# A head's four attention products as split fp32r products among the gate projection's matmuls

## What is computed

```
h = rms_norm(x, attn_norm_g);  proj = h @ w_in      # q,k,v of both kinds, index parts, g_sb, g_ds
# stick-breaking heads
z = q_sb k_sb^T * scale;  mask = key < query
a = where(mask, exp(log_sigmoid(z) + suffix_sum(where(mask, log_sigmoid(-z), 0))), 0)
o_sb = a v_sb
# indexed sparse heads: 64 selected keys of each query
p = softmax(where(selected and causal, qd kd^T * scale, -inf));  o_ds = p v_ds
merged = sigmoid(g_sb) * (o_sb @ w_branch[:1024]) + sigmoid(g_ds) * (o_ds @ w_branch[1024:])
x = x + merged @ w_out;  x = x + MLP(rms_norm(x, ffn_norm_g))
```

## Time and profile before

| | us |
|---|---|
| median of 3 runs | 1435.22 (1435.05 to 1436.7) |
| profiled execution | 1435.36 |
| its span, first to last instruction | 1433.5 |
| PE busy | 1428.1 (100%) |
| DVE busy | 1140.3 (80%) |
| ACT busy | 841.6 (59%) |
| POOL busy | 447.8 (31%) |
| the gates stage: head 0's first chunk begins | at 329.9 |

### The profile page before, as it was taken

One profiled execution on the slowest core, in us unless ns is written; L12 is line 12 of the kernel. 1 busy time (PEld: TensorE's weight loads), 2 busy tenths in 40 slices (PEclk: granted clock), 3 DMA queues, 4 the chain that ended last, 5 costly groups with the idle time before them and its releaser, 6 DMA issues.

```text
span 1433.5 us, 23730 instructions
## 1 busy us (share of the span) xinstructions
PE 1428.1 (100%) x7626; PEld 1223.7 (85%) x7626; DVE 1140.3 (80%) x1533; ACT 841.6 (59%) x1181; POOL 447.8 (31%) x493
## 2 busy tenths in 40 slices
PE   9999999999999999999999999999999999999999
PEld 7888888888888888888888888888888888888887
DVE  6778998886656566899967778777778778999998
ACT  7545667666767666666664455455554545465553
POOL 2310000333132213650025455655556555200000
PEclk9999999999999999999999999999999999999999
DMA  8665665665555555567666666666666665576664
GB/s 255 191 196 173 210 194 183 197 176 176 161 162 158 168 171 178 188 222 233 191 178 182 186 199 182 186 191 190 191 191 180 185 195 189 192 230 206 202 209 147
DMA packets 121064, 272.26 MB, mean 190 GB/s; under 512 B 10688, under 2 KB 10976, under 8 KB 121008
## 3 DMA queue, kind: packets, MB, share of 16 engines
q1 hardware_dynamic: 119936, 268.99, 60.7%
q0 software_dynamic: 896, 2.42, 0.6%
q10 hardware_dynamic: 176, 0.14, 0.0%
HBM read 269.42 MB, written 2.10 MB: 189 GB/s over the span
## 4 chain that ended last, share of the span: by engine, by line
PE 98%; DVE 1%; DMA 0%; issue 0%; ACT 0%; SPq 0%; DVEq 0%; ACTq 0%
PE bank L2086 97%; DVE lo L1215 0%; DMA raw<-in_w_in 0%; PE bank L2140 0%; PE bank L2359 0%; PE bank L2400 0%; DVE y L1758 0%; PE bank L2223 0%; DVE msum L1234 0%; ACT hi L720 0%; SPq L550 0%; DVE msum L1243 0%; DVE msum L1240 0%; DVE lo L1098 0%; ACT hi L637 0%
## 5 line engine op out<-in xcount | busy, mean ns | idle before, releaser
L1098 DVE TENSOR_TENSOR lo<-raw,hi 128x1024 fp32r<-128x1024 f32 (+1 forms) x342 | 444.3, 1304 | 167.1 <-ACT hi L637 166.5
L637 ACT ACTIVATE hi<-raw 128x1024 fp32r<-128x1024 f32 (+1 forms) x342 | 359.2, 1053 | 272.0 <-PE bank L2086 263.8
L2086 PE MATMUL bank<-h2T,hi 128*128 128x512 f32 x1408 | 483.3, 394 | 0.0
L2086 PE MATMUL bank<-h2T,lo 128*128 128x256 f32 x1408 | 376.8, 278 | 0.0
L2086 PEld LDWEIGHTS bank<-h2T,hi 128*128 128x128 f32 x1408 | 257.9, 188 | 53.5
L2086 PE MATMUL bank<-hT,hi 128*128 128x512 f32 (+1 forms) x784 | 272.8, 394 | 0.1
L2086 PEld LDWEIGHTS bank<-h2T,lo 128*128 128x128 f32 x1408 | 264.5, 188 | 7.8
L2086 PE MATMUL bank<-hT,lo 128*128 128x256 f32 (+1 forms) x784 | 212.6, 281 | 0.0
L2050 POOL TENSOR_TENSOR u<-u,rms_row 128x256 f32<-128x256 f32 x88 | 120.8, 1373 | 184.8 <-DVE u L1610 165.8
L2086 PE MATMUL bank<-hi,ffT 128*128 128x512 f32 x576 | 177.3, 389 | 0.0
L2086 PEld LDWEIGHTS bank<-hT,hi 128*128 128x128 f32 (+1 forms) x784 | 143.9, 187 | 29.7 <-DVE lo L1098 0.3
(11 more groups left out here) (298 smaller groups left out, 2023.8 us busy)
## 6 DMA issues: line engine op xcount, KB each, us to landing
raw<-in_w_up SPq DMA_DIRECT2D x176, 512.0 KB, 3.9
raw<-in_w_in SPq DMA_DIRECT2D x160, 512.0 KB, 3.7
raw<-in_w_down SPq DMA_DIRECT2D x88, 512.0 KB, 4.5
raw<-in_w_branch SPq DMA_DIRECT2D x32, 512.0 KB, 3.6
raw<-in_w_out SPq DMA_DIRECT2D x24, 512.0 KB, 5.0
raw4h<-in_w_in SPq DMA_DIRECT2D x8, 512.0 KB, 3.6
raw5h<-in_w_in SPq DMA_DIRECT2D x8, 512.0 KB, 4.0
y<-in_x SPq DMA_DIRECT2D x4, 512.0 KB, 6.5
```

What stands on the lines that cost most here:

```text
L637: act.activation(hi[s][:, 0:width], raw[s][:, 0:width], ACT.Copy)\
L1098: dve.tensor_tensor(lo[s][:, 0:width], raw[s][:, 0:width], hi[s][:, 0:width].bitcast(f32), ALU.subtract)\
L2086: return pe.matmul(o, l, r, start=start, stop=stop, skip_group_check=True)
```

## The change

The four products with fp32 operands become products of fp32r halves, three matmuls in place of each. For this DVE makes the halves: `qk_split(h)` of q and k of both kinds (one copy and one subtraction over 4 x 256 elements; for head 0 ahead of the loop, for head h + 1 in iteration j = 4 of head h), `v_split` (2 x 256 elements, j = 0), `stick_split` (384, ahead of the `lo` of j = 5), `probT_lo` (384, out of PSUM, ahead of the `lo` of j = 6; ACT's `probT` becomes the hi half). POOL no longer copies v, stages into one tile `qk_raw`, and `stage_ds` moves ahead of the mask of `stick`. On PE the blocks behind chunk 0 and chunk 7 go; `cols_chunk` calls `between(k)`, k = 0 to 7, in the middle and at the end of each column tile. In chunk 0 k = 0 to 5 are the scores and logits, in chunk 7 k = 0 to 2 are the first and 5 to 7 the second product with v; each part is one 256-wide and one 128-wide fp32r matmul. The parts at k = 0 wait for the halves. Left out of the diff: semaphore names, and the new `between` parameter in the head of `cols_chunk`.

```diff
@@ -241,15 +241,15 @@
         sin_i = at("sin_i", [TH, 2 * IHALF], A0 + 3968)
         bias = at("bias", [KEYS], A0 + 4096)
         scores = at("scores", [KEYS], A0 + 5632)
-        probT = at("probT", [KEYS], A0 + 5632)
+        probT = at("probT", [KEYS], A0 + 5632, f32r)
 
         W0 = A0 + 7 * KB
         part = [at(f"part{i}", [S], W0 + i * KB) for i in range(4)]
-        sb_q = at("sb_q", [S], W0 + 4 * KB)
-        sb_k = at("sb_k", [S], W0 + 5 * KB)
-        ds_qk = at("ds_qk", [2 * S], W0 + 6 * KB)
-        sb_v = at("sb_v", [TH, HD], W0 + 8 * KB)
-        ds_v = at("ds_v", [TH, HD], W0 + 9 * KB)
+        qk_raw = at("qk_raw", [4, S], W0 + 4 * KB)
+        qk_hi = at("qk_hi", [4, S], 44 * KB, f32r)
+        qk_lo = at("qk_lo", [4, S], 48 * KB, f32r)
+        v_hi = at("v_hi", [2, TH, HD], W0 + 8 * KB, f32r)
+        v_lo = at("v_lo", [2, TH, HD], 52 * KB, f32r)
         partb = [at(f"partb{i}", [S], W0 + (4 + i) * KB) for i in range(4)]
         rms_row = at("rms_row", [S], A0 + 17 * KB)
         one = at("one", [P], A0 + 18 * KB)
...
@@ -317,6 +317,9 @@
         stick = at("stick", [KEYS], 64 * KB + 3072)
         logit = at("logit", [KEYS], 64 * KB + 4608)
         prob = at("prob", [KEYS], 64 * KB + 6144)
+        stick_lo = at("stick_lo", [KEYS], 64 * KB, f32r)
+        stick_hi = at("stick_hi", [KEYS], 64 * KB + 1536, f32r)
+        probT_lo = at("probT_lo", [KEYS], 64 * KB + 6144, f32r)
 
         sig = [[at(f"sig{b}{i}", [S], (32 + 4 * b + i) * KB) for i in range(4)] for b in range(2)]
         br = [[at(f"br{b}{i}", [S], (40 + 4 * b + i) * KB) for i in range(4)] for b in range(2)]
...
@@ -1468,9 +1477,44 @@
             dve.tensor_scalar(bias[:, :], scores[:, :], (NONCAUSAL + TAKEN) / 2, MASKED,
                               ALU.is_gt, ALU.mult).then_inc(bias_raw, 1)
 
-            def gates_body(h):
+            def qk_split(h):
+
+                dve.wait_ge(staged_qk, 3 * h + 3)
+                dve.tensor_copy(qk_hi[:, :, :], qk_raw[:, :, :]).then_inc(qk_hi_done, 1)
+                dve.wait_ge(qk_hi_done, h + 1)
+                dve.tensor_tensor(qk_lo[:, :, :], qk_raw[:, :, :], qk_hi[:, :, :].bitcast(f32),
+                                  ALU.subtract).then_inc(qk_lo_done, 1)
+
+            def v_split(h):
+
+                both = tok[:, 0:4:3, :, ds(HD * h, HD)]
+                dve.tensor_copy(v_hi[:, :, :, :], both).then_inc(v_hi_done, 1)
+                dve.wait_ge(v_hi_done, h + 1)
+                dve.tensor_tensor(v_lo[:, :, :, :], both, v_hi[:, :, :, :].bitcast(f32),
+                                  ALU.subtract).then_inc(v_lo_done, 1)
+
+            def stick_split(h):
+
+                dve.wait_ge(stick_done, h + 1)
+                dve.tensor_copy(stick_hi[:, :], stick[:, :]).then_inc(stick_hi_done, 1)
+                dve.wait_ge(stick_hi_done, h + 1)
+                dve.tensor_tensor(stick_lo[:, :], stick[:, :], stick_hi[:, :].bitcast(f32),
+                                  ALU.subtract).then_inc(stick_lo_done, 1)
+
+            def gates_body(h, more):
                 for j in range(CPG):
+                    if j == 5:
+                        stick_split(h)
+                    if j == 6:
+                        dve.wait_ge(probT_done, h + 1)
+                        dve.tensor_tensor(probT_lo[:, :], B[3][:, 0:KEYS],
+                                          probT[:, :].bitcast(f32), ALU.subtract)\
+                            .then_inc(probT_lo_done, 1)
                     split(C_GATES + AHEAD + j, h, CPG // SLOTS)
+                    if j == 0:
+                        v_split(h)
+                    if j == 4 and more:
+                        qk_split(h + 1)
                     if j == 1:
 
                         dve.wait_ge(logit_full, h + 1)
@@ -1505,8 +1549,10 @@
                                       oT[:, ds(at_head, 1), 0:S].bitcast(f32), ALU.subtract)\
                         .then_inc(done, 1)
 
-            with dve.Fori(0, NH) as h:
-                gates_body(h)
+            qk_split(0)
+            with dve.Fori(0, NH - 1) as h:
+                gates_body(h, True)
+            gates_body(NH - 1, False)
 
             def merged_lo(n, ct):
...
@@ -1949,15 +1995,15 @@
 
             def stage_sb(h):
 
-                pool.tensor_tensor(sb_k[:, :].unsqueeze(1), qkT[:, ds(h, 1), S:2 * S],
+                pool.tensor_tensor(qk_raw[:, 1:2, :], qkT[:, ds(h, 1), S:2 * S],
                                    sb_scale[:, :].unsqueeze(1).to_broadcast([P, 1, S]),
                                    ALU.mult).then_inc(staged_qk, 1)
-                pool.tensor_copy(sb_q[:, :].unsqueeze(1), qkT[:, ds(h, 1), 0:S])\
+                pool.tensor_copy(qk_raw[:, 0:1, :], qkT[:, ds(h, 1), 0:S])\
                     .then_inc(staged_qk, 1)
 
             def stage_ds(h):
-                pool.tensor_copy(ds_qk[:, :].unsqueeze(1), qkT[:, ds(NH + h, 1), :])\
-                    .then_inc(staged_qk, 1)
+                pool.tensor_copy(qk_raw[:, 2:4, :].rearrange("p (n a) s -> p n (a s)", n=1),
+                                 qkT[:, ds(NH + h, 1), :]).then_inc(staged_qk, 1)
 
             with pool.Fori(0, 3) as i:
                 gains_body(i)
@@ -1974,10 +2020,6 @@
                                channel_multiplier=1).then_inc(bias_done, 1)
 
             def head_body(h, more):
-
-                pool.wait_ge(ds_full, 1 + h)
-                pool.tensor_copy(sb_v[:, :, :], tok[:, 0, :, ds(HD * h, HD)]).then_inc(staged_v, 1)
-                pool.tensor_copy(ds_v[:, :, :], tok[:, 3, :, ds(HD * h, HD)]).then_inc(staged_v, 1)
 
                 wait_alone(pool, stay_raw, h + 1)
                 pool.affine_select(out=diagonal(stay), in_=diagonal(stay), compare_op=ALU.is_gt,
@@ -1991,12 +2033,11 @@
 
                     pool.wait_ge(logit_full, h + 1)
                     stage_sb(h + 1)
+                    stage_ds(h + 1)
                 wait_alone(pool, stick_raw, h + 1)
                 pool.affine_select(out=diagonal(stick), in_=diagonal(stick), compare_op=ALU.is_gt,
                                    fill=0.0, base=0, pattern=[[0, 2], [1, P]],
                                    channel_multiplier=-1).then_inc(stick_done, 1)
-                if more:
-                    stage_ds(h + 1)
 
             pool.wait_ge(col_scaled, 4)
...
@@ -2126,9 +2167,14 @@
                                last and j == CK - 1)
                         if first and j == 0:
                             mm(bank[ct][:, 0:S], wl[:, j, cs], src[:, kt, 0:S], False, False)
+                        if between is not None and j == 0:
+                            between(2 * ct)
                     if last and ct < 3:
                         i.then_inc(full, 1)
-                i.then_inc(w_used, 1)
+                    if ct == 3:
+                        i.then_inc(w_used, 1)
+                    if between is not None:
+                        between(2 * ct + 1)
 
             def transposes(k, kts, src, bank=B):
 
@@ -2365,25 +2411,64 @@
             with pe.Fori(1, 4) as i:
                 heads_body(i)
 
+            def split_product(out_, left, right, part, first):
+
+                (l_hi, l_lo), (r_hi, r_lo) = left, right
+                return mm(out_, l_lo if part == 1 else l_hi, r_lo if part == 2 else r_hi,
+                          first and part == 0, part == 2)
+
+            def qk(n, cols):
+                return qk_hi[:, n, cols], qk_lo[:, n, cols]
+
+            def scores_part(h, k):
+
+                old, new, every = slice(0, P), slice(P, S), slice(0, S)
+                if k == 0:
+                    pe.wait_ge(qk_lo_done, h + 1)
+                    pe.wait_ge(qkT_done, 8)
+                if k < 3:
+                    split_product(B[0][:, 0:S], qk(1, old), qk(0, every), k, True)
+                    i = split_product(B[0][:, S:KEYS], qk(1, new), qk(0, new), k, False)
+                    if k == 2:
+                        i.then_inc(z_full, 1)
+                elif k < 6:
+                    split_product(B[1][:, 0:P], qk(2, old), qk(3, old), k - 3, True)
+                    i = split_product(B[1][:, P:KEYS], qk(2, new), qk(3, every), k - 3, False)
+                    if k == 5:
+                        i.then_inc(logit_full, 1)
+
+            def values_part(h, k):
+
+                def product(bank, n, w_hi, w_lo, part):
+                    v = [(v_hi[:, n, t, :], v_lo[:, n, t, :]) for t in range(TH)]
+                    split_product(bank[:, 0:S], v[0], (w_hi[:, 0:S], w_lo[:, 0:S]), part, True)
+                    return split_product(bank[:, P:S], v[1],
+                                         (w_hi[:, S:KEYS], w_lo[:, S:KEYS]), part, False)
+
+                if k == 0:
+                    pe.wait_ge(v_lo_done, h + 1)
+                    pe.wait_ge(stick_lo_done, h + 1)
+                    pe.wait_ge(sb_done, 1 + h)
+                if k < 3:
+                    i = product(B[2], 0, stick_hi, stick_lo, k)
```

(45 more changed lines are left out.)

## The result

The changed kernel takes 1449.0 us (median of 5 runs, 1448.59 to 1450.18) against 1435.22 (5 runs too): ratio 1.0095, 95% interval 1.0084 to 1.0107. That is slower, inside the range and on the forecast's side, 3.5 us above the forecast. The profiled execution is 1448.59, its span 1446.9: +13.4 us on the span of before.

The account below looks back on a forecast made before the run. PE was taken to bound the kernel, by what it issues plus what it waits. Start wait 3.4, products 0.6 and head waits 6.4 gave +10.4 on 1435.36, forecast as 1445.5 us, range 1438.5 to 1449.5.

Parts of the forecast that it names:

- The start wait: Gates stage start: PE's first part waits once for DVE's split of q and k, 3.4 us (3.9 with slow copy).
- The wait in each head: Before each head's transposes: PE waits for POOL's scaling of `prob`, 0.8 us a head, 6.4 in all.
- the step: In each head: PE gives chunk 0 back 1.35 us later, while the transposes' own turn moves by only 0.04.
- Rival B: In the heads POOL gets in before DVE's `lo`, so transposes are just in time; 1439.3 us, chance 0.22.
- The price of the products: On PE, twelve parts of 0.225 us replace fp32 blocks of 2.63: +0.07 a head, +0.6 us in all.
- the upper bound of +0.19: Parts' price on PE if a narrow product costs 0.12 us: +0.19 a head, +1.5 us in all.
- Rival C: On PE weight loads hide, a narrow product costs 0.06; 1434.5 us (chance 0.05), or 1440.9 with head waits (0.03).
- the clock: Behind the 3.4 us start wait the granted clock falls from 2.4 to 1.2 GHz; part of a rival, chance 0.12.
- D: Rival: late `stick` or column sums (+4 us), or slower clock after the start wait (2.8 a chunk); 1450, chance 0.12.
- a slow copy: Gates stage start: DVE's copy of 1,024 elements takes 1.22 us instead of 0.68, making the start wait 3.9.
- waits of 1.0: Upper end of PE's wait for `prob` before each head's transposes, estimated at 0.55 to 1.0 us.
- The work beside: DVE's 4.4 us more a head, POOL's stagings and SP's weight loads cost nothing, least margin 0.9 us.

Follow-up runs that it names:

- the third experiment: Changed kernel, with DVE holding back its fifth `lo` of a head until POOL has scaled `prob`; 1444.03 us, ratio 1.0062.
- the second profile: The changed kernel run and profiled once more with no edit; 1449.09 us, ratio 1.0095, span 1447.3.
- the first profile: The profiled execution of the changed kernel's own measurement; 1448.59 us, span 1446.9.
- the blocks: Changed kernel with the same fp32r parts in a row as two blocks behind chunks 0 and 7; 1440.36 us, ratio 1.0033.
- the order: Changed kernel with the 128-wide product put ahead of the 256-wide one in the later parts; 1450.2 us, ratio 1.01.
- the three together: Changed kernel with score parts in chunk 1, narrow products first in later parts, and head 0's halves made earlier; 1439.77 us, ratio 1.003.
- the first hybrid: Changed kernel with 128-wide products as single fp32 products, 256-wide ones still split, score parts in chunk 1, head 0's halves earlier; 1435.29 us, ratio 0.9998.
- the fourth experiment: Changed kernel with every 128-wide product of a part made 256 wide, which alters the attention's values; 1449.73 us, ratio 1.0101.
- one digit: Changed kernel with the score parts set in chunk 1 instead of chunk 0; 1439.01 us, ratio 1.0024.

## Why the prediction was right, and where its sum was off

**The start wait** (3.4 us) is 3.4: 334.86 - 331.37 = 3.49 from the last `lo` less its own 0.12. By the terms, the copy has a row of 0.68, as estimated, and counts 0.61 in the chain because it starts under the end of `bias`; the subtraction took 1.32 (1.22).

**The wait in each head** (0.8) came by the mechanism forecast, in all eight heads, and cost 0.70, of which 0.67 is the wait. ACT's second `hi` starts when chunk 0 is used, with an idle gap ahead (1.10), `lo` follows `stay_lo` at once (402.43 - 401.98 = 0.45, of the 0.54), and POOL takes 2.67 where 2.55 was expected. From that `hi` to the end of POOL's work it is 404.94 - 392.69 = 12.25, was 11.56: +0.69. From that `hi` to where the transposes could have begun it is 404.33 - 392.69 = 11.64, was 12.75: -1.11, where the step had -1.31; the 0.20 between is the wider spacing, which brings the transposes later. (The recorded start of the fifth `hi`, 394.25, should be 392.75 + 0.51 + 1.08 = 394.34 by its own terms; nothing hangs on it.) Rival B (POOL first) was what the third experiment made by force: no wait at all, as it said. By the Trainium skill ("SBUF — State Buffer", "Who interferes with whom") the one issued second waits for the whole of the first. POOL's side agrees: 2.67 with the `lo` beside it, 1.63 with the `lo` held back. DVE's side shows less: with POOL's second scaling under way from 395.08 to 396.00, the `lo` from 395.18 took 1.46, 0.24 more than 1.22 and not 0.82 more, so "the whole of the first" isn't borne out there.

**The price of the products** is the term that was mis-sized: +0.07 a head was +0.20, 1.6 us in all. The narrow product was taken at 0.11; it costs what a wide one does, 2.83 / 24 = 0.118 each. Its 0.06 under a long product was the wrong row, its 0.12 the right one, and the upper bound of +0.19 was the value. The Trainium skill ("TensorE: Matmul & The Clock Gate", "Back-to-back issue gap") has 81 ns for 128 columns; no row here shows it, and the sum by it, 2.2 us faster, was far off. Rival C falls with it: the weight loads don't hide.

**Not foreseen**: the wider spacing behind the parts, 0.20 a head or 1.6 us. **Foreseen as a rival only**: the clock. D's 2.8 us for each slow chunk was 1.56 in the second profile. The term that the first profile has in its place, 1.2 us before the stage, doesn't come with the change: the same instructions ran without it.

The sum by its own terms, for the first profile: 3.4 (3.4 forecast) + 1.6 (0.6) + 5.6 (6.4) + 1.6 (0) + 1.2 (0) = 13.4 (10.4). For the second: 1.6 of clock in place of the 1.2, 13.8. So the mechanism was right, and the number is inside the range partly by luck. The median is 3.5 above the forecast and 0.5 below the range's upper end, and the spacing (1.6) was in no term, the clock (1.6) only in a rival with a chance of 0.12: D said 1450, and 1449.0 is nearer to that than to 1445.5. The upper end had room for them because it took in a slow copy and waits of 1.0, which didn't come.

The work beside (DVE's 4.4 us more a head, POOL's staging, SP's loads) cost nothing, as forecast: PE's rows show no other wait in the stage.

**What stays open**: what makes the spacing 0.353 instead of 0.347. It appears behind sequences of fp32r products with weights of their own, not behind the same with all 256 wide, and in every head it is gone behind the transposes (in the changed kernel 16 pairs from 378.67 to 384.23, 0.3475 each). It is in the branch stage of some kernels (90.1 to 90.2 with the blocks, the order, the three together and the first hybrid; 88.9 in the others). In three of these four a 256-wide fp32r product stands last ahead of the stage, in the fourth a block does; but the kernel with all products 256 wide has 88.9, so that is no rule yet. A transpose ended it in one kernel, and an fp32 product put last kept it out of another. Whether weight loads and products run out of step there was not shown, only argued. It was not tried to reset it in the middle of the changed kernel's heads; the fourth experiment says that the wait would take the gain.

## What to carry to other kernels

Count a small matmul with weights of its own by its weight load and not by its columns (here 0.118 us for 128 and for 256 columns alike): three split products in place of an fp32 one gain where they are 256 wide (3 x 0.118 = 0.35 against 0.43) and lose where they are 128 wide (0.35 against 0.22), so choose by shape. Setting products among others moves when their chunk is given back and when their operands are wanted; look for who waits for that chunk, and put the products where that chain has slack (one digit gave 10 us). A wait at a stage's start costs more than itself where the granted clock falls behind it.

## What the runs showed that was not expected

- PE's pairs have two spacings at a granted clock of 1.00, 0.347 and 0.353 us in the heads, set by the products ahead and kept through a stage of 90 us (1.2 us there); a single transpose switched it back.
- A wait of 3.4 us of PE was followed by a stretch at 0.66 to 0.72 granted clock in three of five profiles of kernels that have it; kernels with 1.8 us or less showed 1.00.
- 1.2 us were lost at 22 us into the program in one profile of the changed kernel and not in the other, with the same instructions; a late weight load stands behind it.
